# An mLSTM mixer whose head norm moves into the output weights and into its last product

## The chip, the cores and the metric

The kernel runs on one core of one Trainium2 chip. The metric is the device time of one execution in microseconds. The tensor engine (PE in the profile) has a queue of its own, as have VectorE (DVE), ScalarE (ACT), GpSimd (POOL) and SyncE (SP, which only issues loads here). They meet through semaphores alone, and each runs its own instructions in the order in which they are written. The matmuls are float32 products cut into parts: every operand x is held as a rounded high part and the rest, x = hi + lo, and three matmuls (hi·lo, lo·hi, hi·hi) stand for one.

## The reference, cut to what matters

The program is a stack of feed-forward blocks and four mixers over 256 tokens of width 1024. The change is in the first mixer, `mlstm_mixer`, which has 8 heads of 128 values each:

```python
h = h + 0.5 * swiglu(rmsnorm(h, ...), ...)               # block before
proj = rmsnorm(h, g) @ w_in                              # q, k, v, input and forget gates, output gate og
# ... decay weights W (256 x 256 per head, causal), num and den per head ...
h_out = num / jnp.maximum(jnp.abs(den), jnp.exp(-m_t))[..., None]
h_out = rmsnorm(h_out, g_head).reshape(B, T, H * M_DV)   # norm over the 128 values of each head
return (h_out * jax.nn.sigmoid(og)) @ w_out              # added to h; the next block follows
```

So for head j and token t the input of the last matmul is num · (share 1/max(|den|, floor)) · (root of the head) · g_head · sigmoid(og).

## The kernel before, in words

**Weights.** All weights pass through 7 slots in pieces of up to 128 x 2048. SP loads a piece when the slot is free (`used`, counted by PE after the last matmul on a piece); ACT writes its high part (`hi`, L1520, a copy to the rounded type), DVE its low part (`lo`, L2047, raw minus high). `split_to(p)` on either engine means "bring the parts of all pieces before p". Where it stands in an engine's program decides what waits behind 1.9 us (ACT) or 2.2 us (DVE) of it. The four pieces of the output matrix `a_w_out` are `first` to `first + 3`; piece i holds the rows of heads 2i and 2i + 1.

**Tokens.** There are two halves of 128 tokens, t = 0 and 1. Inputs of a matmul are turned by PE (a matmul with the identity), then ACT writes XH (`x_hi`) and DVE XL (`x_lo`).

**The first mixer on PE** (L1032 to L1126): chunks 0 to 2 of the projection; chunk 3 (96 matmuls of 256 columns, four column tiles m = 0 to 3); six small turns of the gate sums (`m_a`, `m_floor`, L1044); `rows_of_heads` (L1052), which DVE's `m_a` must precede; chunk 4; the scores of heads 0 to 3; the output gate's first product `og_products(5, 0, 7)`; the numerators of heads 0 to 3; scores 4 to 7; `og_products(6, 0, 7)`; numerators 4 to 7; the output gate of t = 1 (`og_products(5, 1, 2)` and `(6, 1, 3)`); `turn_heads(0)`, which waits for the finished heads of t = 0; and `out_stage`, eight parts of 12 matmuls of 512 columns (four pieces, t = 0 then t = 1), with `turn_heads(1)` after the second part. Then the second feed-forward block (`ffn1`) begins.

**On DVE** (L2341 to L2433): `values_in(2)`, `m_a`, the decay (L2353), the weights of each head (`m_weights`, L2369 and L2371), `numerators_in(g)` for four heads at a time (three small operations on shares and one product of 1024 elements from PSUM, L2387), `head_sums` (L2394: sums of the squares), `og_gain` (L2400: sigmoid(og) times g_head, 1024 elements), `mean_square` and `root` (11 small operations, L2077 and L2062 to L2072, for all 16 columns), `heads(t)` (L2408: eight products of 128 elements), and the `lo` pieces between them.

**On ACT** (L1707 to L1740): the decay's sigmoids, the `hi` pieces, `og_in` (the sigmoid of a gate product, L1723), `head_squares` (two Squares of 1024 elements, L1728), `x_hi` (L1548).

**On POOL**: the broadcast of g_head to 128 x 1024 (L645), and the causal zeros in the decay (L650).

Of the kernel before, what the change touches and what calls it, by code (L numbers as in the profile page):

```python
# [23 lines left out]
P = 128  # L24
# [82 lines left out]
def program(nc, a, out):  # L107
# [32 lines left out]
    NP = len(pieces)  # L140

    with ExitStack() as ctx:
# [60 lines left out]
        def carve(start, *sizes):  # L203
            views, at = [], start
            for n in sizes:
# [6 lines left out]
        m_qT, m_kT, m_v, m_og, m_E, m_g, m_tok, m_gain = carve(0, 1024, 1024, NT * HEADS * 129, 2048, HEADS * 384, 32, 80,  # L212
                                                                   1024)
# [9 lines left out]
        m_a = m_tok[:, 0:16].rearrange("p (t h) -> p t h", t=NT)  # L223
        m_floor = m_tok[:, 16:32].rearrange("p (t h) -> p t h", t=NT)
# [113 lines left out]
        og_dve = sem("og_dve")  # L338
        gain_in = sem("gain_in")
# [45 lines left out]
        roots = ["ffn0", "mlstm", "head", "ffn1", "kv", "keys", "kcmp", "nsa", "q0", "q1", "ffn3", "ln00", "ln01", "ckv",  # L385
# [241 lines left out]
        def _(pool):  # L627
# [17 lines left out]
            pool.dma_start(m_gain, a["a_g_head"].rearrange("l h d -> l (h d)")[0:1, :].to_broadcast([P, D])).then_inc(gain_in, 16)  # L645
# [28 lines left out]
        def _(pe):  # L674
# [57 lines left out]
            def turn_heads(t):  # L732

                pe.wait_ge(heads_ready, t + 1)
                for w in range(2):
                    for k in range(4):
                        last = tr(PS[:, turn_bank("mlstm_out", t, w), k * P:k * P + P],
                                  xs[:, t, (4 * w + k) * P:(4 * w + k) * P + P], ident)
                    last.then_inc(turned, 1)
# [195 lines left out]
            def out_stage(name, between=None):  # L935

                for t in range(NT):
                    if name != "mlstm_out":
                        pe.wait_ge(z_ready, 2 * zstage[name[:3]] + t + 1)
                    for i in range(4):  # L940
                        out_part(name, t, i)
                        if t == 0 and i == 1 and between:
                            between()
# [99 lines left out]
            chunk("mlstm", 3)  # L1043
            for name, sums in (("m_a", (grow[2], grow[0])), ("m_floor", (grow[1],))):  # L1044
                o = side(name)
                pe.wait_ge(side_src, src_no[name])
                for i, row in enumerate(sums):
                    for t in range(NT):
                        last = tr(o[:, 16 * i + 8 * t:16 * i + 8 * t + 8], row[:, t * P:t * P + P], con[0:HEADS, 0:HEADS])
                last.then_inc(side_ps, 1)  # L1050
# [41 lines left out]
            def og_products(c, t, bank):  # L1092

                n, end = stages["mlstm"][1][c][2], chunk_end("mlstm", c)
                for i, p in enumerate((end - 2, end - 1)):
# [6 lines left out]
                    if t == 1:  # L1102
                        last.then_inc(used, 1)
                if t == 0:
                    last.then_inc(og_ps, 1)
# [403 lines left out]
        def _(act):  # L1509
# [10 lines left out]
            def hi(p, n=PIECE):  # L1520

                act.wait_ge(landed[p % SLOTS], 32 * (p // SLOTS + 1))
                A(whi[:, p % SLOTS, 0:n], raw[:, p % SLOTS, 0:n], ACT.Copy).then_inc(hi_done, 1)  # L1523
# [15 lines left out]
            def x_hi(name, t):  # L1539

                for w in range(2):
# [171 lines left out]
            first = first_piece["mlstm_out"]  # L1713
# [11 lines left out]
            def head_squares(g, to):  # L1725
# [310 lines left out]
        def _(dve):  # L2036
# [391 lines left out]
            for w in range(2):  # L2428
                x_lo("mlstm_out", 0, w)
# [542 lines left out]
```

## Time and profile before

| | us |
|---|---|
| median of 3 runs (lowest, highest) | 1315.61 (1312.67, 1315.66) |
| span of the profiled execution | 1310.3 |
| PE busy in that span | 1270.2 |
| DVE busy | 873.9 |
| ACT busy | 613.6 |

The span runs from the first to the last instruction; the device time also holds what lies around it. The profiled execution's own device time is not printed: between its span and the three times lie 2.4 to 5.4 us. The first mixer takes some 110 us of the span, from about 203 to 317 us.

### The profile page before, as it was taken

The page shows a single profiled execution, that of the slowest core. Times are in us where ns is not written, and L with a number is a line of the kernel's source. Part 1 is how long each engine was busy: PE and PEld are TensorE (multiplying, and loading weights), DVE is VectorE, ACT ScalarE, POOL GpSimd, SP SyncE. Part 2 cuts the span into 40 slices and gives each one's busy share as a digit, 9 for nine tenths or more (in the row PEclk, how much of TensorE's full clock was granted, in tenths as well). Part 3 has the DMA queues.
Part 4 walks back from the last instruction along what each step waited for, and adds up shares of the span by engine and source line. Part 5 has one row for each costly group of instructions (what it writes and reads, how often), then busy time and mean ns, then how long its engine had stood idle before and what let it go on. Part 6 is the DMA issues. An engine that isn't in the chain of part 4 may idle for free.

```text
span 1310.3 us, 16491 instructions
## 1 busy us (share of the span) xinstructions
PE 1270.2 (97%) x6717; PEld 1077.6 (82%) x6717; DVE 873.9 (67%) x1312; ACT 613.6 (47%) x839; POOL 24.2 (2%) x37
## 2 busy tenths in 40 slices
PE   6999999989999999999999999999999999999997
PEld 5888888988788888878888886778888899988876
DVE  6655557885755556685657569856555567566896
ACT  6444346435434445444435357654444344544461
POOL 2000000100000000000000000000000000000000
PEclk9999999999999999999999989999999999999999
DMA  9655545443555556565665440065666686446401
GB/s 329 207 182 187 186 162 185 142 155 129 183 184 185 188 192 186 166 193 170 217 224 169 159 161 1 1 200 187 191 193 193 130 217 172 150 130 211 176 2 65
DMA packets 158812, 218.17 MB, mean 167 GB/s; under 512 B 8257, under 2 KB 110993, under 8 KB 158737
## 3 DMA queue, kind: packets, MB, share of 16 engines
q1 hardware_dynamic: 156880, 212.56, 51.2%
q0 software_dynamic: 1376, 3.71, 0.9%
q8 instruction: 53, 0.87, 0.3%
q10 hardware_dynamic: 480, 0.85, 0.2%
q14 instruction: 23, 0.18, 0.0%
HBM read 216.04 MB, written 1.05 MB: 166 GB/s over the span
## 4 chain that ended last, share of the span: by engine, by line
PE 82%; DVE 11%; issue 3%; ACT 2%; SPq 1%; DMA 1%; DVEq 0%
PE PS L686 23%; PE PS L689 23%; PE PS L687 23%; DVE wlo L2050 2%; PE PS L823 1%; PE PS L721 1%; PE PS L722 1%; ACT whi L1523 1%; PE PS L706 1%; PE PS L1300 1%; DVE arena L2639 1%; PE PS L728 1%; PE PS L1016 1%; SPq L591 1%; DVE XL L2090 1%
## 5 line engine op out<-in xcount | busy, mean ns | idle before, releaser
L2050 DVE TENSOR_TENSOR wlo<-raw,whi 128x2048 fp32r<-128x2048 f32 (+4 forms) x206 | 457.4, 2230 | 122.6 <-ACT whi L1523 121.8
L1523 ACT ACTIVATE whi<-raw 128x2048 fp32r<-128x2048 f32 (+4 forms) x206 | 381.4, 1863 | 63.4 <-DMA raw<-in_fox_w_in_dram 33.1
L686 PE MATMUL PS<-whi,XL 128*128 128x512 f32 (+3 forms) x992 | 385.8, 390 | 8.9 <-DVE scr L2152 3.8
L687 PE MATMUL PS<-wlo,XH 128*128 128x512 f32 (+3 forms) x992 | 379.8, 384 | 0.0
L689 PE MATMUL PS<-whi,XH 128*128 128x512 f32 (+3 forms) x992 | 265.0, 384 | 0.0
L686 PEld LDWEIGHTS PS<-whi,XL 128*128 128x128 f32 x992 | 187.3, 189 | 45.1 <-DVE scr L2152 4.9
L689 PEld LDWEIGHTS PS<-whi,XH 128*128 128x128 f32 x992 | 185.5, 190 | 35.5
L687 PEld LDWEIGHTS PS<-wlo,XH 128*128 128x128 f32 x992 | 187.4, 189 | 32.9
L1577 ACT ACTIVATE scr<-PS,rn 128x256 f32<-128x256 f32 x88 | 41.7, 474 | 225.2 <-PE PS L689 223.9
L686 PE MATMUL PS<-whi,GL 128*128 128x512 f32 x320 | 125.4, 392 | 0.0
L687 PE MATMUL PS<-wlo,GH 128*128 128x512 f32 x320 | 124.6, 389 | 0.0
L2149 DVE SCALAR_TENSOR_TENSOR scr<-PS,rn,scr 128x256 f32<-128x256 f32 x88 | 42.5, 483 | 92.8 <-ACT scr L1577 92.8
L1582 ACT ACTIVATE GH<-PS 128x512 fp32r<-128x512 f32 x40 | 23.9, 599 | 167.1 <-PE PS L823 167.1
L689 PE MATMUL PS<-whi,GH 128*128 128x512 f32 x320 | 98.7, 390 | 0.0
L686 PE MATMUL PS<-XH,wlo 128*128 128x256 f32 x320 | 81.4, 287 | 1.2 <-ACT xs L2017 1.2
L2158 DVE TENSOR_TENSOR GL<-PS,GH 128x512 fp32r<-128x512 f32 x40 | 27.7, 692 | 79.5 <-ACT GH L1582 79.4
L687 PE MATMUL PS<-XL,whi 128*128 128x256 f32 x320 | 80.2, 283 | 0.0
L689 PEld LDWEIGHTS PS<-whi,GH 128*128 128x128 f32 x320 | 60.1, 188 | 12.6
L687 PEld LDWEIGHTS PS<-wlo,GH 128*128 128x128 f32 x320 | 60.1, 188 | 12.1
L686 PEld LDWEIGHTS PS<-whi,GL 128*128 128x128 f32 x320 | 60.1, 188 | 12.2
L686 PEld LDWEIGHTS PS<-XH,wlo 128*128 128x128 f32 x320 | 61.3, 192 | 2.8 <-ACT xs L2017 2.0
L687 PEld LDWEIGHTS PS<-XL,whi 128*128 128x128 f32 x320 | 61.3, 192 | 0.1
(387 smaller groups left out, 1339.2 us busy)
## 6 DMA issues: line engine op xcount, KB each, us to landing
raw<-in_ffn_w_in_dram SPq DMA_DIRECT2D x174, 512.0 KB, 5.0
raw<-in_ffn_w_out_dram SPq DMA_DIRECT2D x88, 512.0 KB, 4.9
raw<-in_fox_w_in_dram SPq DMA_DIRECT2D x24, 512.0 KB, 7.9
raw<-in_a_w_in_dram SPq DMA_DIRECT2D x16, 512.0 KB, 4.6
raw<-in_dsa_w_in_dram SPq DMA_DIRECT2D x16, 512.0 KB, 6.0
raw<-in_kv_w_dram SPq DMA_DIRECT2D x12, 512.0 KB, 4.2
raw<-in_fox_w_in_dram SPq DMA_DIRECT2D x12, 344.0 KB, 5.0
raw<-in_a_w_out_dram SPq DMA_DIRECT2D x8, 512.0 KB, 4.9
```

The costliest lines, as they stand in the source:

```text
L591: sp.dma_start(dst[:, :, w, :], w_in[:, 4 * half:4 * half + 4, w, FC * i:FC * i + FC])\
L686: mm(o, xl, wh, start=start and i == 0, stop=False, skip_group_check=True)
L687: mm(o, xh, wl, start=False, stop=False, skip_group_check=True)
L689: last = mm(o, xh, wh, start=False, stop=stop and i == len(terms) - 1, skip_group_check=True)
L706: last = tr(PS[:, turn_bank(name, t, w), k * P:k * P + P], h[:, t, (4 * w + k) * P:(4 * w + k) * P + P], ident)
L721: mm(o, xh, wl, start=opens and i == 0 and j == 0, stop=False, skip_group_check=True)
L1523: A(whi[:, p % SLOTS, 0:n], raw[:, p % SLOTS, 0:n], ACT.Copy).then_inc(hi_done, 1)
L1577: A(ffe[:, t, :], PS[:, 4 + t, 0:FC], ACT.Sigmoid, scale=rn[:, t:t + 1]).then_inc(exp_done, 1)
L1582: A(to[:, :, :].rearrange("p k t -> p (k t)"), PS[:, 6, :], ACT.Copy).then_inc(gh_done, 1)
L2050: V.tensor_tensor(wlo[:, p % SLOTS, 0:n], raw[:, p % SLOTS, 0:n], whi[:, p % SLOTS, 0:n].bitcast(F32), ALU.subtract).then_inc(lo_done, 1)
L2149: V.scalar_tensor_tensor(out=g, in0=PS[:, 4 + t, 0:FC], scalar=rn[:, t:t + 1], in1=e, op0=ALU.mult, op1=ALU.mult).then_inc(silu_step, 1)
L2158: V.tensor_tensor(to[:, :, :], two(PS[:, 6, :]), hi_[:, :, :].bitcast(F32), ALU.subtract)\
```

## The change

The gain g_head is no longer multiplied into the gate. It scales the rows of the output matrix while its high and low parts are made (two operations of 1024 elements, one per head of the piece, in place of one of 2048), so `og_gain` and POOL's broadcast go. The squares are summed by ACT as it makes them (16 operations of 128 elements with an accumulator output, instead of two of 1024), so `head_sums` goes. The second four heads are squared from PSUM with the share as scale, and are no longer written out by `numerators_in(1)`: the last product reads them from PSUM, with share times root as its scalar. The root is taken per token half. The heads of t = 0 are turned four at a time: the first four in the middle of `og_products(6, 1, 3)`, the second four after the first part of `out_stage`; those of t = 1 after its third part. Some further steps are moved: `values_in(2)` ahead of the `lo` pieces, the gate sums' turns into chunk 3 (after tile m = 2), the parts of piece `first` ahead of the scores, and the first gate product ahead of a wait for the last decay. The banks into which heads are turned change from 4 to 7 to 2 to 5.

```diff
+    row_gains = {first_piece["mlstm_out"] + i: R_HEAD + 2 * i for i in range(4)}
...
             if name == "mlstm_out":
-                return 4 + 2 * t + w
+                return 2 + 2 * t + w
...
-            pool.dma_start(m_gain, a["a_g_head"].rearrange("l h d -> l (h d)")[0:1, :].to_broadcast([P, D])).then_inc(gain_in, 16)
...
+            def turn_heads(t, w):
+                pe.wait_ge(heads_ready, 4 if t else w + 1)
+                if t == 0:
+                    pe.wait_ge(og_act, 3 + w)
+                for k in range(4):
+                    last = tr(PS[:, turn_bank("mlstm_out", t, w), k * P:k * P + P],
+                              xs[:, t, (4 * w + k) * P:(4 * w + k) * P + P], ident)
+                last.then_inc(turned, 1)
...
+            pe.wait_ge(side_act, looks(side_no["m_M2"], "act"))
+            og_products(5, 0, 7)
             pe.wait_ge(side_act, looks(side_no["m_M3"], "act"))
-            og_products(5, 0, 7)
...
-            og_products(6, 1, 3)
-            turn_heads(0)
-            out_stage("mlstm_out", lambda: turn_heads(1))
+            og_products(6, 1, 3, lambda: turn_heads(0, 0))
...
+            out_stage("mlstm_out", {0: lambda: turn_heads(0, 1), 2: second_heads})
...
# ScalarE
+                if p in row_gains:
+                    for k in range(2):
+                        part = slice(D * k, D * k + D)
+                        last = A(whi[:, p % SLOTS, part], raw[:, p % SLOTS, part], ACT.Identity,
+                                 scale=par[:, row_gains[p] + k:row_gains[p] + k + 1])
...
             A(m_kT[:, 0:2, :], two(o), ACT.Copy).then_inc(chunk_act, 1)
+            first = first_piece["mlstm_out"]
+            split_to(first + 1)
             decay(2)
...
+                for j in range(4):
+                    hh, c = 4 * g + j, 8 * t + 4 * g + j
+                    if g == 0:
+                        src, by = xs[:, t, hh * P:hh * P + P], 1.0
+                    else:
+                        src, by = PS[:, 4 + j, t * T:t * T + P], m_shares[g][:, j, t:t + 1]
+                    last = A(m_squares[g][:, t, j * P:j * P + P], src, ACT.Square, scale=by, accum_out=ss[:, c:c + 1])
+                last.then_inc(head_sq, 1)
...
# VectorE
+                        last = V.scalar_tensor_tensor(
+                            out=wlo[:, p % SLOTS, part], in0=raw[:, p % SLOTS, part],
+                            scalar=par[:, row_gains[p] + k:row_gains[p] + k + 1],
+                            in1=whi[:, p % SLOTS, part].bitcast(F32), op0=ALU.mult, op1=ALU.subtract)
...
+            def head_root(t):
+                dve.wait_ge(head_sq, 3 + t)
+                mean_square(8, P, EPS, ss[:, 8 * t:8 * t + 8])
+                root(f"head{t}", 8, rr[:, 8 * t:8 * t + 8])
...
+                for g in range(2):
+                    if g:
+                        dve.wait_ge(head_sq, 4)
+                        fours = rr[:, 8 * t + 4:8 * t + 8]
+                        link(V.tensor_tensor(fours, fours, m_shares[1][:, :, t], ALU.mult))
+                    for j in range(4):
...
+                                                      in0=PS[:, 4 + j, t * T:t * T + P] if g else xs[:, t, cols],
+                                                      scalar=rr[:, c:c + 1], in1=m_og[:, t, cols],
...
+                    last.then_inc(heads_ready, 1)
...
-            head_sums(0)
+            shares(1).then_inc(m_out, 1)
+            dve.wait_ge(m_out, 2)
+            head_root(0)
+            heads(0)
+            x_lo("mlstm_out", 0, 0)
+            head_root(1)
             split_to(first + 3)
-            og_gain(0)
-            numerators_in(1)
-            head_sums(1)
-            mean_square(16, P, EPS)
-            root("head", 16)
-            heads(0)
-            og_gain(1)
-            for w in range(2):
-                x_lo("mlstm_out", 0, w)
+            x_lo("mlstm_out", 0, 1)
             heads(1)
```

DVE while PE works on chunk 3, kernel before (L2050 are `lo` pieces, L2287 is `values_in(2)`, L2343 and L2344 are `m_a`):

```order
L2050 TENSOR_TENSOR wlo<-raw,whi 128x2048 x2
L2287 TENSOR_SCALAR arena<-PS,r 128x4x128
L2343 TENSOR_SCALAR arena<-PS 128x16
L2344 TENSOR_SCALAR arena<-PS 128x16
L2050 TENSOR_TENSOR wlo<-raw,whi 128x1536 x2
```

The same place in the changed kernel (L2088 is `lo`, L2328 `values_in`, L2385 and L2386 `m_a`):

```order
L2328 TENSOR_SCALAR arena<-PS,r 128x4x128
L2088 TENSOR_TENSOR wlo<-raw,whi 128x2048
L2385 TENSOR_SCALAR arena<-PS 128x16
L2386 TENSOR_SCALAR arena<-PS 128x16
L2088 TENSOR_TENSOR wlo<-raw,whi 128x2048
L2088 TENSOR_TENSOR wlo<-raw,whi 128x1536 x2
```

One `lo` piece of 2048 has moved behind `m_a`.

DVE from the second four numerators to the heads of t = 0, kernel before (the root's ten operations are left out in the middle):

```order
L2050 TENSOR_TENSOR wlo<-raw,whi 128x2048
L2400 TENSOR_TENSOR arena<-arena 128x1024
...
L2386 RECIPROCAL arena<-arena 128x8
L2387 TENSOR_TENSOR xs<-PS,arena 128x4x2x128
L2394 TENSOR_REDUCE ss<-arena 128x2x4
L2077 TENSOR_SCALAR rv<-ss 128x16
...
L2072 SCALAR_TENSOR_TENSOR rr<-rt,ry 128x16
L2408 SCALAR_TENSOR_TENSOR xs<-xs,rr,arena 128x128 x8
L2400 TENSOR_TENSOR arena<-arena 128x1024
L2097 TENSOR_TENSOR XL<-PS,XH 128x4x128 x2
```

The same stretch in the changed kernel (L2082 is `lo` of an output piece, L2451 share times root, L2135 `x_lo`):

```order
L2082 SCALAR_TENSOR_TENSOR wlo<-raw,par,whi 128x1024 x2
...
L2428 RECIPROCAL arena<-arena 128x8
L2115 TENSOR_SCALAR rv<-ss 128x8
...
L2110 SCALAR_TENSOR_TENSOR rr<-rt,ry 128x8
L2456 SCALAR_TENSOR_TENSOR xs<-xs,rr,arena 128x128 x4
L2451 TENSOR_TENSOR rr<-rr,arena 128x4
L2456 SCALAR_TENSOR_TENSOR xs<-PS,rr,arena 128x128 x4
L2135 TENSOR_TENSOR XL<-PS,XH 128x4x128
```

Between the shares and the heads nothing is left but the root; the `lo` piece that stood there, and a second root, come behind.

PE at the end of the gate products, changed kernel (L736 are the turns of the heads; before, all eight stood in one row behind the last matmul of 384 columns):

```order
L687 MATMUL PS<-whi,XH 128x384 x4
L736 MATMUL PS<-con,xs 128x128 x4
L684 MATMUL PS<-whi,XL 128x384
...
L687 MATMUL PS<-whi,XH 128x384 x4
L684 MATMUL PS<-whi,XL 128x512
...
L687 MATMUL PS<-whi,XH 128x512 x2
L736 MATMUL PS<-con,xs 128x128 x4
```

Twelve gate matmuls now stand between the first four turns and the output products, and twelve output matmuls between the first and the second four turns.

## Rows read from the trace of the kernel before

**Rows 1.** Page, part 1: busy time, share of the span, instructions.
```profile
PE 1270.2 (97%) x6717; PEld 1077.6 (82%) x6717; DVE 873.9 (67%) x1312; ACT 613.6 (47%) x839; POOL 24.2 (2%) x37
```

**Rows 2.** PE's waits, 240 to 335 us: total, times, longest.
```profile
PE PS L737 <- DVE xs L2408: 2.5, 1, 2.5
PE PS L1058 <- DVE arena L2344: 1.0, 1, 1.0
PE PS L686 <- DVE XL L2097: 0.7, 1, 0.7
PE PS L686 <- ACT arena L1703: 0.6, 1, 0.6
PE PS L1087 <- DVE arena L2371: 0.4, 1, 0.4
PE PS L686 <- DVE xs L2387: 0.3, 1, 0.3
```

**Rows 3.** Windows: length, PE, PEld, DVE, ACT, POOL busy, PEclk, DMA share, GB/s.
```profile
287.00:290.00 3.00, 0.53 (x5) 0.40 (x5) 2.93 (x11) 0.58 (x1) 0.00 (x0) 0.99 1.01 348
...
292.00:296.00 4.00, 4.00 (x10) 3.17 (x11) 4.00 (x10) 1.70 (x1) 0.00 (x0) 0.50 0.66 212
296.00:300.00 4.00, 4.00 (x19) 3.24 (x18) 0.93 (x1) 0.00 (x0) 0.00 (x0) 0.90 0.00 0
```

**Rows 4.** PE in order of time: start, us, instruction, idle before.
```profile
232.54 0.28 PE L686 MATMUL PS<-XH,wlo 128*128 128x256 f32 x1
...
261.94 0.44 PE L686 MATMUL PS<-whi,XL 128*128 128x384 f32 x1 [0.62 <-ACT arena L1703]
262.22 0.33 PE L687 MATMUL PS<-wlo,XH 128*128 128x384 f32 x1
...
289.60 1.66 PE L737 MATMUL PS<-con,xs 128*128 128x128 f32 x8 [2.47 <-DVE xs L2408]
291.92 0.77 PE L686 MATMUL PS<-whi,XL 128*128 128x512 f32 x1 [0.65 <-DVE XL L2097]
...
298.38 0.39 PE L686 MATMUL PS<-whi,XL 128*128 128x512 f32 x1
298.61 0.39 PE L687 MATMUL PS<-wlo,XH 128*128 128x512 f32 x1
...
299.75 1.04 PE L737 MATMUL PS<-con,xs 128*128 128x128 f32 x8
```

**Rows 5.** DVE in order of time.
```profile
263.79 2.29 DVE L2050 TENSOR_TENSOR wlo<-raw,whi 128x2048 fp32r<-128x2048 f32 x1 [0.56 <-ACT whi L1523]
...
279.81 1.22 DVE L2400 TENSOR_TENSOR arena<-arena 128x1024 f32<-128x1024 f32 x1
...
285.18 0.17 DVE L2077 TENSOR_SCALAR rv<-ss 128x16 f32<-128x16 f32 x1
...
287.35 2.19 DVE L2408 SCALAR_TENSOR_TENSOR xs<-xs,rr,arena 128x128 f32<-128x128 f32 x8
```

**Rows 6.** ACT in order of time.
```profile
271.67 1.06 ACT L1728 ACTIVATE scr<-xs 128x1024 f32<-128x1024 f32 x1 [4.66 <-DVE xs L2387]
...
784.34 0.36 ACT L1862 ACTIVATE arena<-PS,nmin 128x128 f32<-128x128 f32 x1
784.68 0.37 ACT L1862 ACTIVATE arena<-PS,nmin 128x128 f32<-128x128 f32 x1
```

**Rows 7.** Groups by form: busy us, mean ns of one, idle before.
```profile
L1624 ACT ACTIVATE arena<-arena,nmin 128x128 f32<-128x128 f32 x16 | 6.2, 390 | 6.1 <-DVE nmin L2205 6.0
L2246 DVE SCALAR_TENSOR_TENSOR xs<-h,lns,arena 128x1024 f32<-128x1024 f32 x4 | 5.1, 1286 | 3.1 <-DMA arena<-in_ln_b_dram 3.0
L2371 DVE SCALAR_TENSOR_TENSOR arena<-PS,arena 128x128 f32<-128x128 f32 x8 | 2.7, 342 | 0.0
```

**Rows 8.** DVE and PE at the start of the next block, in order of time.
```profile
309.93 1.28 DVE L2120 SCALAR_TENSOR_TENSOR h<-PS,h 128x512 f32<-128x512 f32 x2
314.25 1.04 PE L706 MATMUL PS<-con,h 128*128 128x128 f32 x8
```

More of the change, by code:

```diff
@@ L223, in program @@
         m_a = m_tok[:, 0:16].rearrange("p (t h) -> p t h", t=NT)
+        m_shares = [m_tok[:, 32 + 8 * g:40 + 8 * g].rearrange("p (h t) -> p h t", h=4) for g in range(2)]
         m_floor = m_tok[:, 16:32].rearrange("p (t h) -> p t h", t=NT)
@@ L933, in out_part, with out_stage @@
                         last.then_inc(acc_done, 1)
-            def out_stage(name, between=None):
+            def out_stage(name, between={}):
                 for t in range(NT):
@@ L941, in out_stage @@
                         out_part(name, t, i)
-                        if t == 0 and i == 1 and between:
-                            between()
+                        if t == 0 and i in between:
+                            between[i]()
                         if t == 1 and i == 2 and name in then_turns:
@@ L1042, in _, with sums_turned @@
             chunk("mlstm", 2)
[L1043 to L1050, printed above, removed]
+            def sums_turned():
+                for name, sums in (("m_a", (grow[2], grow[0])), ("m_floor", (grow[1],))):
+                    o = side(name)
+                    pe.wait_ge(side_src, src_no[name])
+                    for i, row in enumerate(sums):
+                        for t in range(NT):
+                            last = tr(o[:, 16 * i + 8 * t:16 * i + 8 * t + 8], row[:, t * P:t * P + P], con[0:HEADS, 0:HEADS])
+                    last.then_inc(side_ps, 1)
+            chunk("mlstm", 3, None, {2: sums_turned})
             def rows_of_heads(name, j):
@@ L1103, in og_products @@
                         last.then_inc(used, 1)
+                    if between and i == 0:
+                        between()
                 if t == 0:
@@ L2049, in lo @@
                 dve.wait_ge(hi_done, p + 1)
+                if p in row_gains:
+                    for k in range(2):
+                        part = slice(D * k, D * k + D)
+                        last = V.scalar_tensor_tensor(
+                            out=wlo[:, p % SLOTS, part], in0=raw[:, p % SLOTS, part],
+                            scalar=par[:, row_gains[p] + k:row_gains[p] + k + 1],
+                            in1=whi[:, p % SLOTS, part].bitcast(F32), op0=ALU.mult, op1=ALU.subtract)
+                    last.then_inc(lo_done, 1)
+                    return
                 V.tensor_tensor(wlo[:, p % SLOTS, 0:n], raw[:, p % SLOTS, 0:n], whi[:, p % SLOTS, 0:n].bitcast(F32),
@@ L2396, in og_gain @@
-            def og_gain(t):
-                dve.wait_ge(og_act, 2 * t + 2)
-                dve.wait_ge(gain_in, 16)
-                V.tensor_tensor(m_og[:, t, :], m_og[:, t, :], m_gain, ALU.mult).then_inc(og_dve, 1)
-            def heads(t):
-                dve.wait_ge(og_dve, t + 1)
-                for hh in range(HEADS):
-                    cols = slice(hh * P, hh * P + P)
-                    c = 8 * t + hh
-                    last = V.scalar_tensor_tensor(out=xs[:, t, cols], in0=xs[:, t, cols], scalar=rr[:, c:c + 1],
-                                                  in1=m_og[:, t, cols], op0=ALU.mult, op1=ALU.mult)
-                last.then_inc(heads_ready, 1)
@@ L2412, in _, with first_numerators @@
-            split_to(first + 1)
+                return V.reciprocal(rd, rd)
+            def first_numerators():
+                link(shares(0))
+                V.tensor_tensor(xs[:, :, 0:512].rearrange("p t (h d) -> p t h d", h=4),
+                                PS[:, 4:8, :].rearrange("p h (t n) -> p t h n", t=NT)[:, :, :, 0:P],
+                                m_shares[0].rearrange("p h t -> p t h").unsqueeze(3).to_broadcast([P, NT, 4, P]),
+                                ALU.mult).then_inc(m_out, 1)
```

69 lines of the change are left out of this document (34 added, 35 removed).

## The prediction

> **What bounds the kernel now.** First the busy shares: PE is busy for 97% of the span [rows 1]. So a change that leaves PE's instructions as they are, as this one does (the same products, 16 turns of 128 x 128 in another place), can give back only PE's idle time and time at a low clock. The page's groups don't show where that lies, so I read the waits next, in the stretch of the first mixer. PE waits there six times, 5.5 us in all [rows 2]: 2.5 for the heads of t = 0 (L737), 1.0 for `m_a` (L1058), 0.7 for XL ahead of the first output product, 0.6 for the last decay ahead of the first gate product, 0.4 for the first head's weights (L1087), 0.3 for the first numerators. The third view is the windows [rows 3]: the longest wait falls in 287 to 290 us; in 292 to 296 PE ran at half the clock (0.50, its 1.2 GHz level), in 296 to 300 at 0.90 on average. The fourth is PE in order of time [rows 4], which puts a price on this. The first eight turns took 1.66 us, the second eight 1.04. The 24 products between 291.92 and 299.75 took 7.83 us; at the spacing of 0.23 us that they have once the clock is back (298.38 to 298.61) they would take 5.4. So the wait of 2.47 cost 0.6 + 2.4 = 3.0 us more through the clock. No other wait of rows 2 was followed by this.
>
> **The profiled execution and the median.** The sums are made in the span of 1310.3 us. The median of 1315.6 is 5.3 above it, the lowest time 2.4. I take off from the median what I take off from the span.
>
> **What each removed wait is worth.** The five waits that the change aims at: 2.47 + 1.03 + 0.65 + 0.62 + 0.41 = 5.2 us. Each also costs PE its pipelining: a matmul of 0.39 us starts 0.23 after the one before, so 0.16 us of overlap is lost, and the first after a wait is longer (0.44 against 0.33 [rows 4]); 0.25 each, 1.2 in all. With the clock's 3.0 the most that can come is 9.4 us. The wait of 0.3 for the first numerators stays: same operations, same order.
>
> **Do the waits really go?** I lay the changed kernel out with PE as the clock, from the start of chunk 3 at 232.5 [rows 4], without waits unless one is found. The spacing is 0.23 us for 512 columns [rows 4], and in proportion 0.17 for 384, 0.12 for 256 and 0.11 for 128, by the eight turns at 299.75 (1.04 less 0.16 of overlap, over 8). Three tiles of chunk 3 end at 241.3, the six small turns at 242.0, the fourth tile at 244.9; rows of heads 245.8, chunk 4 257.5, rows of heads 258.4, scores 260.2, gate product 264.3, numerators and scores 268.7, the kept wait 269.0, gate product 273.2, numerators 276.0, 36 gate products 282.0, four turns and 12 gate products 284.5, output part 287.2, four turns and two parts 293.1, eight turns 294.0.
>
> *The gate sums.* `m_a` comes behind one `lo` piece, where two stood (2.2 us each [rows 5]), and PE turns the sums inside chunk 3, at 241.3. `m_a` ends at 243.4, PE asks for it at 244.9. Behind it the moved piece (second half of chunk 4) is ready at 245.6, asked for at 247.3. The wait of 1.03 goes.
>
> *The early output piece.* Parts of piece `first` (2.2 to 2.5 us on DVE) move ahead of the key copy L2360, into DVE's idle time before it. Queued behind it is that copy, which the scores wait for: it ends at 258.3, PE is there at 258.4. No slack, but no cost; were it 0.5 late, 0.5 is lost. In exchange the head weights start as soon as the decays are done (261.9 instead of 266.0), so the 0.41 goes; and the gate product no longer waits for the fourth decay, so the 0.62 goes.
>
> *The squares.* ACT now runs 16 Squares with accumulator. Nearest rows: L1862, the same size from PSUM with an accumulator, starts every 0.34 us (784.34 to 784.68 [rows 6]); L1624 from SBUF lasts 0.39, and its readout lies beside the next [rows 7]. Lower bound 0.34; upper bound one old Square of 1024 elements, 1.06 [rows 6]. I take 0.38 from SBUF, 0.36 from PSUM. The first eight (3.1 us) and a `hi` piece (now 2 x about 1.05, by L1728's 1.06 for 1024 elements) stand ahead of `og_in(6, 0)`, which numerator 7 waits for: from 269.0, 3.1 + 2.1 + 0.5 gives 274.8; PE asks at 275.2. Hidden with 0.4 to spare.
>
> The Trainium skill (VectorE: DVE Perf Modes, on the TRN2 errata) says that ScalarE pays a fixed 224 cycles per instruction from SBUF and 172 from PSUM, and advises against tiles under 512 elements, which speaks against 16 small squares for two large ones. By its formula one costs 0.29 us (352 cycles at 1.2 GHz) before the readout of the accumulator. The rows' 0.34 to 0.39 hold the readout, so the sum would be the same; the advice would only bite if ACT had no idle time here.
>
> *The chain to the heads.* Before: `lo` piece, `og_gain` 1.2, numerators, Square 1.1 [rows 6], `head_sums` (1024 elements like `og_gain`), root of 11 operations from 285.18 to 287.35 (2.2), eight products 2.2 [rows 5]. Now from numerator 7's end at 276.0: shares 0.6, four PSUM squares 1.5, root 2.2 (its operations are bound by their fixed part: 0.17 us for 16 columns), four products 1.1: 281.7. PE asks after 36 gate products of 0.17, at 282.0. Slack 0.3. The second four need the other squares (279.9), the share product (0.2) and four products from PSUM (L2371 from PSUM 0.34, like L2408 from SBUF): 283.0, asked for at 287.2. The first output product asks for XL at 284.5, there at 284.0. So 2.47 and 0.65 go, and with them the half clock: PE has no wait over 0.4 us from 232 to past 320.
>
> *The gained parts* of the output pieces on DVE: nearest rows 1.22 (L2400, 1024 elements [rows 5]) and 1.29 (L2246, three operands [rows 7]), less 0.1 of overlap: 2.3 to 2.5 a piece instead of 2.2. Piece `first + 3` stands behind both heads(1) and the second root; DVE works without a pause from 278.3 to about 294.3. PE asks for it at 294.0. Here I expect a wait of 0.3 us (0 to 0.9 by these bounds).
>
> The Trainium skill (same page, same section) gives VectorE 120 fixed cycles from PSUM against 58 from SBUF. The eight products that now read PSUM would be longer by 62 cycles, 0.065 us, each: 0.5 us on DVE's full stretch, and the wait here 0.8. The rows don't bear it out (0.342 from PSUM, 0.348 from SBUF), so I leave it out of the sum.
>
> *The next block.* Before, DVE's updates of h begin at 309.93 and end 3.0 us ahead of PE's turns at 314.25 [rows 8]. PE gains on DVE, since the three `lo` pieces between still follow the `hi` pieces. I get 304.6 for DVE and 305.2 for PE, so the cover shrinks to under a us.
>
> *POOL's broadcast* of 0.5 MB runs early, at 32 us, where no wait of PE is; nothing.
>
> Sum: 9.4 - 0.3 (last output piece) - 0.3 (half of the chance that one of the three places with under 0.4 us of slack is missed by 0.6) = 8.8 us. Nothing behind the first mixer is tied to absolute time, so the gain stays.
>
> **The rivals.**
> - *DVE becomes the bound at the seams.* If gained parts and products are at their upper bounds, waits of 0.9 at the last output piece, 0.5 at the key copy, 0.3 at the first turns and up to 1 at the turns of the next block come back, none long enough to lower the clock if the rows are a guide (1.03 did not). Gain about 9.4 - 2.7 = 6.7: 1309. For it: DVE's full stretch; against: every price has a near row.
> - *The long wait only shrinks.* If squares take 0.6 each, numerator 7 waits 1.3 and the first turns 0.6. If a wait near 2 remains (at 0.75), the clock falls again: gain 9.4 - 3.0 - 2.5 - 1 = 3: 1312.6.
> - *Slower: the squares on ACT.* It is one mechanism: ACT's queue holds eight squares ahead of `og_in(6, 0)` and eight ahead of `og_in(5, 1)`. At 1.0 us a square, near the upper bound, numerator 7 waits 8 x 0.62 - 0.4 = 4.5 us and the turns of the first heads, which also wait for `og_in(5, 1)`, 3.3. Each wait is longer than the 2.47 that brought half clock, so 3.0 comes twice. Against the 9.4: 7.8 + 6.0 = 13.8, so 4.4 slower: 1320. It decides from about 0.8 us a square. Against it: rows 6 and 7 have the same size at less than half of that.
> - *It doesn't do what it says: given back later.* The weights for the next block come with all DMA queues busy (share 1.01 [rows 3]). If their loads, not PE, set its start, PE only waits there instead. Against: the loads follow PE's own `used`, and four pieces of 1 MB, whose slots come free from 278 on, take 3 us each at 350 GB/s: the last lands at about 292 and is wanted at 308. No change: 1315.5.
>
> **How the numbers follow.** Forecast 0.63 (1304.5 to 1308.8), DVE at the seams 0.20, the wait that shrinks 0.08, slower 0.04, given back 0.05. The likeliest gives 1315.6 - 8.8 = 1306.8. Range 1303 to 1312: the low end is the full 9.4 and the 3 us by which the three times before differ; the high end takes in the seams and most of the shrunken wait. Under 0.3% (3.9 us) a measurement of this kernel can't tell a change from none. Faster by more: 0.63 + 0.20 + 0.02 = 0.85. Within: 0.06 + 0.05 = 0.11. Slower: 0.04.
>
> **What would show it.** Right: PE clock 1.00 through 287 to 300; no PE wait over 0.5 us on the heads' turns, on `m_a` or on the decay; PE's first output product about 7 us earlier; Squares of 128 elements starting every 0.34 to 0.40 us. Wrong: a PE wait of over 2 us anywhere between 260 and 310; numerator 7 waiting for ACT; a stretch of PE at 0.50; or a shorter mixer and a next block that waits for DMA.

## The result, and the profile after

The changed kernel takes 1302.5 us (median of four, 1301.3 to 1303.1); the kernel before took 1314.9 in the runs beside it (1312.7 to 1315.7). The ratio of the runs is 0.9921, with a 95% interval of 0.9903 to 0.9939 (the quotient of the two medians, 0.9906, lies inside it). Later, on another chip with more runs, it was 1303.2 against 1312.1: 0.993 (0.9916 to 0.9945). So it is faster by 0.7 to 0.8%, and the two intervals leave 0.6 to 1.0%. The span went from 1310.3 to 1299.6.

Page, part 1, of the kernel after. PE has the same 6717 matmuls [rows 1], is busy for 3.8 us less (for the most part the half clock, which had stretched the mixer's matmuls by about 2.8, below) and idle for less; DVE and ACT hardly changed.

```profile
PE 1266.4 (97%) x6717; PEld 1075.7 (83%) x6717; DVE 870.9 (67%) x1324; ACT 617.9 (48%) x873; POOL 24.5 (2%) x36
```

PE's waits, 230 to 345 us, after (the stretch that holds those of [rows 2]): us in total, times, longest.

```profile
PE PS L684 <- DVE scr L2190: 0.9, 1, 0.9
PE PS L684 <- DVE xs L2433: 0.3, 1, 0.3
```

All five waits that the prediction set out to remove are gone. The 0.3 for the first numerators stayed, as forecast. The 0.9 lies in the next block, after 318 us, and stood there before the change too: the stretch of [rows 2] holds this seventh wait as well, 0.89 us at 330.71, which those rows leave out. The windows over the heads, which answer to [rows 3], have PE busy throughout at a granted clock of 1.00:

```profile
280.00:283.00 3.00, 3.00 (x21) 2.97 (x20) 2.33 (x9) 0.60 (x1) 0.00 (x0) 1.00 0.95 297
283.00:286.00 3.00, 3.00 (x15) 2.48 (x14) 2.69 (x12) 0.58 (x1) 0.00 (x0) 1.00 1.01 340
286.00:290.00 4.00, 4.00 (x21) 3.32 (x20) 3.85 (x12) 2.68 (x3) 0.00 (x0) 1.00 1.09 358
```

PE in order of time, for [rows 4]. Subtract 1.95 us from any time of before to compare: chunk 3 starts that much earlier, for a reason that lies at the start of the program (below).

```profile
230.59 0.28 PE L684 MATMUL PS<-XH,wlo 128*128 128x256 f32 x1
...
258.44 0.45 PE L684 MATMUL PS<-whi,XL 128*128 128x384 f32 x1
...
280.75 0.60 PE L736 MATMUL PS<-con,xs 128*128 128x128 f32 x4
...
283.28 0.39 PE L684 MATMUL PS<-whi,XL 128*128 128x512 f32 x1
...
291.98 1.03 PE L736 MATMUL PS<-con,xs 128*128 128x128 f32 x8
292.77 0.47 PE L684 MATMUL PS<-whi,XL 128*128 128x512 f32 x1
```

The first output product starts 8.6 us earlier than in [rows 4], and the eight last turns 7.8. Less the shift that is 6.7 (about 7 was the sign of being right) and 5.8.

DVE and ACT, after, for [rows 5] and [rows 6]: the root of t = 0 begins at 276.95, behind the last of its PSUM squares; the products of `heads` that read their numbers from PSUM cost the same as those from SBUF.

```profile
276.95 0.17 DVE L2115 TENSOR_SCALAR rv<-ss 128x8 f32<-128x8 f32 x1 [1.64 <-ACT arena L1753]
...
279.04 1.14 DVE L2456 SCALAR_TENSOR_TENSOR xs<-xs,rr,arena 128x128 f32<-128x128 f32 x4
...
280.29 1.13 DVE L2456 SCALAR_TENSOR_TENSOR xs<-PS,rr,arena 128x128 f32<-128x128 f32 x4
282.02 0.69 DVE L2135 TENSOR_TENSOR XL<-PS,XH 128x512 fp32r<-128x512 f32 x1 [0.61 <-ACT XH L1566]
...
290.20 2.47 DVE L2082 SCALAR_TENSOR_TENSOR wlo<-raw,par,whi 128x1024 fp32r<-128x1024 f32 x2
```
```profile
267.51 0.31 ACT L1753 ACTIVATE scr<-xs 128x128 f32<-128x128 f32 x1 [3.99 <-DVE xs L2433]
...
267.82 0.29 ACT L1753 ACTIVATE scr<-xs 128x128 f32<-128x128 f32 x1
268.02 0.19 ACT L1753 ACTIVATION_READ_ACCUMULATOR scr<-xs 128x1 f32 x1
268.11 0.29 ACT L1753 ACTIVATE scr<-xs 128x128 f32<-128x128 f32 x1
...
275.34 0.37 ACT L1753 ACTIVATE arena<-PS,arena 128x128 f32<-128x128 f32 x1 [2.73 <-DVE arena L2428]
...
275.70 0.36 ACT L1753 ACTIVATE arena<-PS,arena 128x128 f32<-128x128 f32 x1
```

A square starts every 0.29 us from SBUF and every 0.34 to 0.36 from PSUM.

**One measure for every trace below.** The *mixer stretch* is PE's time from the start of chunk 3 (232.54 in [rows 4]) to the first turn of gated values in the next feed-forward block (336.30 there): before 103.76, after 325.82 - 230.59 = 95.23. So the mixer gave 8.53 us, where 8.8 was forecast. The span fell by 10.7. Of the other 2.2, 1.98 had arisen by 33 us, at the first such turn of the first block (33.34 before, 31.36 after).

### The profile page after: what moved, and what is told of

Read it like the earlier page. It is cut to its first block, busy times and chain, and to the rows that moved or that the text cites. A ratio compares the mean times of both kernels' runs of the same rounds, so it can differ in the third digit from the quotient of the medians.

```text
span 1299.6 us, 16537 instructions
## 1 busy us (share of the span) xinstructions
PE 1266.4 (97%) x6717; PEld 1075.7 (83%) x6717; DVE 870.9 (67%) x1324; ACT 617.9 (48%) x873; POOL 24.5 (2%) x36
## 4 chain that ended last, share of the span: by engine, by line
PE 86%; DVE 9%; issue 2%; ACT 2%; SPq 1%; DMA 1%; DVEq 0%
PE PS L684 25%; PE PS L687 25%; PE PS L685 24%; PE PS L822 1%; PE PS L719 1%; PE PS L720 1%; DVE wlo L2088 1%; PE PS L726 1%; PE PS L704 1%; PE PS L1015 1%; PE PS L1311 1%; DVE arena L2685 1%; SPq L590 1%; DMA raw<-in_ffn_w_out_dram 1%; DVE d_work L2934 1%
## 5 line engine op out<-in xcount | busy, mean ns | idle before, releaser
L2088 DVE TENSOR_TENSOR wlo<-raw,whi 128x2048 fp32r<-128x2048 f32 (+4 forms) x202 | 448.2, 2229 | 121.2 <-ACT whi L1541 120.5
L1541 ACT ACTIVATE whi<-raw 128x2048 fp32r<-128x2048 f32 (+4 forms) x202 | 373.8, 1862 | 61.9 <-DMA raw<-in_fox_w_in_dram 32.7
L684 PE MATMUL PS<-whi,XL 128*128 128x512 f32 (+3 forms) x992 | 384.5, 388 | 6.6 <-DVE scr L2190 2.7
L684 PEld LDWEIGHTS PS<-whi,XL 128*128 128x128 f32 x992 | 186.4, 188 | 42.0 <-DVE scr L2190 3.9
L684 PE MATMUL PS<-whi,GL 128*128 128x512 f32 x320 | 125.4, 392 | 0.0
L684 PE MATMUL PS<-XH,wlo 128*128 128x256 f32 x320 | 81.5, 287 | 1.2 <-ACT xs L2046 1.2
L684 PEld LDWEIGHTS PS<-whi,GL 128*128 128x128 f32 x320 | 60.1, 188 | 12.2
L684 PEld LDWEIGHTS PS<-XH,wlo 128*128 128x128 f32 x320 | 61.3, 191 | 2.9 <-ACT xs L2046 2.0
```

The costliest lines, as they stand in the source:

```text
L684: mm(o, xl, wh, start=start and i == 0, stop=False, skip_group_check=True)
L2088: V.tensor_tensor(wlo[:, p % SLOTS, 0:n], raw[:, p % SLOTS, 0:n], whi[:, p % SLOTS, 0:n].bitcast(F32), ALU.subtract).then_inc(lo_done, 1)
```

## The experiments

Spans are of one profiled execution each. From the first block's turn to chunk 3, all fourteen traces agree within 0.05 us (199.18 to 199.23), so the mixer stretch can be read to better than 0.1: the two traces of before differ by 0.02, the two of after by 0.04. The two ends of the program can't: up to the first turn took 31.3 to 33.3, and all behind the stretch 972.6 to 976.0.

The far end goes with the clock. Between the mixer and the last 15 us, where all but root first have the same instructions, early moves only and delay four show no half clock and took 972.6 and 972.7; the four traces with one such stretch of 6.8 us took 973.7 to 974.0, and the seven with two stretches 974.8 to 976.0. (Root first has one of 3.4 and took 972.7, with its own saving in it.) Which of them a trace has does not follow the kernel: after has one, after again two.

| kernel | up to first turn | mixer stretch | waits in it beyond those of after | rest of the difference |
|---|---|---|---|---|
| before | 33.34 | 103.76 | 5.18 | 3.35 |
| before, again | 31.34 | 103.78 | 5.25 | 3.30 |
| after | 31.36 | 95.23 | 0 | 0 |
| after, again | 31.85 | 95.19 | 0 | 0 |
| broadcast back | 31.45 | 95.21 | 0 | 0 |
| early moves only | 31.48 | 100.71 | 3.51 | 1.97 |
| heads only | 31.88 | 97.89 | 2.53 | 0.13 |
| delay, three | 31.29 | 96.96 | 1.49 | 0.24 |
| delay, four | 31.32 | 98.17 | 2.76 | 0.18 |
| two waits | 31.45 | 101.87 | 3.45 | 3.19 |
| one longer | 31.92 | 102.04 | 4.01 | 2.80 |
| turns together | 31.79 | 97.06 | 1.28 | 0.55 |
| gain in the gate | 32.19 | 96.26 | 0.79 | 0.24 |
| root first | 31.57 | 94.04 | -0.87 | -0.32 |

The last column is the stretch less 95.23 less the waits: refilling PE, and the clock.

**1. The changed kernel again.**

> The changed kernel once more, with a second profile. My theory: the first mixer alone gave 8.5 us (PE from the start of chunk 3 to the first turn of the next block's gates: 95.2 us against 103.8), and the 2 us by which the changed kernel was already ahead at 33 us are chance, since no changed instruction of PE lies there. Then 95.2 within 0.2 again, and the stretch 0 to 33 us may fall either way by 2 us; ratio 0.990 to 0.994. Rival (the start belongs to the change): the changed kernel is again 2 us ahead at 33 us, and PE never drops to half clock at 28 us.

Measured: stretch 95.19, ratio 0.993; the first turn came at 31.85, with the clock at 1.00 from 10 to 34 us. That is as the theory has it for the mixer. For the start it leaves the rival standing, since 31.85 is again 1.5 ahead of the one trace of before; experiment 5 decides it.

**2. The broadcast back.** The gains are loaded again, and only waited for, not used:

```diff
+            pool.dma_start(m_gain, a["a_g_head"]...to_broadcast([P, D])).then_inc(gain_in, 16)
...
                 dve.wait_ge(og_act, 2 * t + 2)
+                dve.wait_ge(gain_in, 16)
```

> The changed kernel with POOL's 0.5 MB broadcast of the head gains put back into the start (loaded, not used). Theory: it costs nothing: time within 1 us of the changed kernel beside it, mixer stretch 95.2. Rival (the broadcast held the loads at the start up): 2 us slower than the changed kernel, PE at half clock near 28 us as in the kernel before.

Measured: 1302.7 against 1303.2 for the changed kernel on the same chip, stretch 95.21, first turn at 31.45. The broadcast costs nothing, as predicted, and its absence did not bring the 2 us at the start.

**3. The early moves alone.**

> The kernel before with only the moves in the early part: values of a chunk taken before its split piece, the sums turned inside chunk 3, the first output piece split ahead of the key copy, the gate product behind M2. Theory: the waits of 1.03, 0.62 and 0.41 us go, 2.1 us, with next to nothing for refills; the heads are not faster, so their wait stays near 2.5 and the half clock behind it too: mixer stretch 103.8 - 2.1 = 101.7, about 2 us faster than before. Rival (the waits are one chain: what is removed early comes back at the heads): the wait for the heads grows to 4.5 and the stretch stays at 103.8. By my recorded sum with 0.25 a refill it would be 2.8.

Measured: 1307.1 against 1312.1, ratio 0.9966 (0.9953 to 0.9979); the stretch is 100.71, so 3.05 gained where I expected 2.1. The waits on `m_a`, the decay and the first weights are gone, and the one for the heads kept its size:

```profile
PE PS L737 <- DVE xs L2419: 2.4, 1, 2.4
PE PS L686 <- DVE XL L2103: 1.1, 1, 1.1
PE PS L686 <- DVE scr L2158: 0.9, 1, 0.9
PE PS L686 <- DVE xs L2398: 0.3, 1, 0.3
```

So the rival of one chain falls: what was taken away early did not come back at the heads, apart from 0.4 us at XL. The surplus over 2.1 is in the clock: the waits in the stretch are 1.67 less than before, and the other 1.38 stands in the last column of the table, nearly all of it clock (the three refills saved are about 0.13). Windows of this kernel show PE at half clock from 288.0 to 291.4 only, 3.4 us, where it was 6.8 in the kernel before ([rows 3] has 0.50 throughout 292 to 296):

```profile
284.00:288.00 4.00, 1.40 (x10) 1.15 (x10) 3.76 (x9) 1.77 (x3) 0.00 (x0) 1.00 1.07 358
288.00:292.00 4.00, 4.00 (x12) 3.13 (x11) 4.00 (x10) 1.11 (x1) 0.00 (x0) 0.57 0.66 210
292.00:296.00 4.00, 4.00 (x24) 3.35 (x23) 0.44 (x1) 0.50 (x2) 0.00 (x0) 1.00 0.00 0
```

**4. The heads alone.**

> The changed kernel with the early moves undone: only the heads' part stays (gain in the output weights, squares with accumulator on ACT, root and gate by half, turns within the last gate product). Theory: the waits of 1.03, 0.62 and 0.41 are back, no wait for the heads over 0.5 and no half clock: stretch 95.2 + 2.1 = 97.3, about 6.4 faster than before. If both parts add, this and the early moves alone sum to 8.5. Rival (the later start of the head weights, by the `first` piece of 2.3 us on DVE, reaches the heads): wait of over 1 us at the heads' turns, stretch 99 or more.

Measured: 1306.3 against 1312.1, ratio 0.9954 (0.9938 to 0.9971); stretch 97.89, 5.87 gained, no half clock. There was no wait for the heads, so the rival falls. The wait for the first weights was 0.9 instead of 0.4, since the late `first` piece has its gain now and the weights stand behind it: most of the 0.6 by which it missed 97.3. DVE's half of the piece is 0.2 longer than in [rows 5], and ACT's high part comes later, so DVE waits 0.84 for it and not 0.56:

```profile
262.60 2.48 DVE L2081 SCALAR_TENSOR_TENSOR wlo<-raw,par,whi 128x1024 fp32r<-128x1024 f32 x2 [0.84 <-ACT whi L1537]
```

The two parts give 3.05 + 5.87 = 8.92, and 8.53 together. So the early moves are worth 3.05 on the kernel before, some 1.25 of it by a shorter half clock, and 8.53 - 5.87 = 2.66 on top of the heads' part.

**5. The kernel before again**, for the start.

> The kernel before once more, for a second trace. At 33 us it was 1.5 to 2.0 us behind the four other kernels (33.3 against 31.4 to 31.9 at the first turn of the first block's gates), and one of those four has the broadcast and none of the heads' part. Theory: that was chance, it comes at 31.4 to 31.9 now; the mixer stretch is 103.8 again. Rival: it belongs to the kernel before, 33.3 again.

Measured: first turn at 31.34, stretch 103.78. The 2 us at the start were chance. Windows of the first trace of before and then of this one: in the first PE had waited 1.97 us for gated values, and ran at half clock from 27.1 to 30.6; here the same wait was 1.3, and the clock stayed at 1.00.

```profile
24.00:27.00 3.00, 1.03 (x6) 0.70 (x5) 2.62 (x4) 2.27 (x3) 0.00 (x0) 1.00 1.10 349
27.00:31.00 4.00, 4.00 (x12) 3.13 (x11) 3.96 (x4) 1.07 (x2) 0.00 (x0) 0.57 1.08 376
```
```profile
24.00:27.00 3.00, 1.74 (x8) 1.19 (x7) 2.64 (x4) 2.27 (x3) 0.00 (x0) 1.00 1.10 348
27.00:31.00 4.00, 4.00 (x19) 3.31 (x18) 3.96 (x5) 0.66 (x2) 0.00 (x0) 1.00 1.07 374
```

**6 and 7. A wait of chosen length at the first turns.** On DVE, before the root of t = 0, n operations that keep the gate's values (n = 3, then 4; one trace each):

```diff
             dve.wait_ge(m_out, 2)
+            dve.wait_ge(og_act, 2)
+            for _ in range(n):
+                link(V.tensor_tensor(m_og[:, 0, :], m_og[:, 0, :], m_og[:, 0, :], ALU.max))
             head_root(0)
```

> The changed kernel with three extra 1024-element operations (1.2 us each; they leave the values as they are) on DVE before the root of t = 0. DVE has 1.64 us idle there and the turns have about 0.6 of slack, so PE waits about 1.4 us at the first turns. Theory (the clock falls only behind a long wait): stretch 95.2 + 1.4 + at most 0.6 at XL = 96.6 to 97.2, clock 1.00 throughout. Rival (any wait of over 1 us at this place costs the half clock): 98 or more.

> The same with four: PE waits about 2.6 us at the first turns. Theory: half clock behind it as in the kernel before: 95.2 + 2.6 + 1.7 to 3.0 = 99.5 to 100.8. Rival (the half clock came from the two waits of 2.5 and 0.65 close together, or was chance): clock stays 1.00, 97.8.

Measured: 1.49 us of wait and a stretch of 96.96; 2.76 us and 98.17. The first is as expected, the second is not: my theory that a wait of this length always brings half clock fell, and the rival's 97.8 with the clock at 1.00 is near. Windows of the kernel with four:

```profile
281.00:284.00 3.00, 0.40 (x4) 0.40 (x5) 2.73 (x14) 0.00 (x0) 0.00 (x0) 1.00 0.90 269
284.00:288.00 4.00, 4.00 (x23) 3.69 (x22) 3.52 (x17) 1.19 (x2) 0.00 (x0) 1.00 1.00 329
```

**8 and 9. Two waits close together, or one longer.** The second theory, from the traces so far, was that the second wait (0.65 us, at XL [rows 2]) was needed too.

> The changed kernel with four extra operations on DVE before the root of t = 0 and two more before its first XL (values kept): PE waits 2.8 us at the first turns, as it did with four alone, and 1.6 more at the first output product, 2.7 us of work later. In both traces of the kernel before and in the one with only the early moves, the half clock came behind two waits close together (2.5 and 0.65, or 2.4 and 1.1); a single 2.8 left the clock alone. Theory: two waits close together bring it: 95.2 + 2.8 + 1.6 = 99.6 for the waits and 1.3 to 3.0 on top, 101 to 102.6. Rival (the place or chance decides): clock 1.00, 99.6.

> The changed kernel with five extra operations before the root of t = 0 and none at XL: one wait of 4.0 us. If the sum of idle time in such a stretch decides (2.5 + 0.65 is more than 2.8), the half clock comes here too: 95.2 + 4.0 + 1.3 to 3.0 = 100.5 to 102.2. If it takes two waits, the clock stays 1.00: 99.2 to 99.4.

Measured: 101.87 and 102.04, both with half clock, and both in the range of their theories. But PE in the kernel with two waits, and the windows behind it, show that the theory of two waits falls as well:

```profile
283.73 0.66 PE L736 MATMUL PS<-con,xs 128*128 128x128 f32 x4 [2.75 <-DVE xs L2456]
288.29 0.77 PE L684 MATMUL PS<-whi,XL 128*128 128x512 f32 x1 [0.70 <-DVE XL L2135]
```
```profile
281.00:283.00 2.00, 0.00 (x0) 0.00 (x0) 1.73 (x11) 0.00 (x0) 0.00 (x0) 1.00 0.99 327
283.00:285.00 2.00, 1.27 (x9) 1.27 (x10) 1.93 (x9) 0.58 (x1) 0.00 (x0) 1.00 1.03 317
285.00:287.00 2.00, 2.00 (x8) 2.00 (x7) 1.97 (x2) 0.02 (x1) 0.00 (x0) 0.50 1.08 374
```

The second wait is 0.70 and not the planned 1.6, since PE at half clock comes to it later (3.9 us behind the start of the first turns, where after has 2.5). The clock fell at 285.0, 2.6 us before the second wait begins. Up to there this kernel and the one with four operations do the same on PE, with waits of 2.75 and 2.76, and one lost its clock and the other kept it. In both traces of the kernel before the clock also fell ahead of the wait for XL. So neither the length of a wait of this size nor a second one decides; a wait of 2.45 to 2.76 us brought the half clock four times out of five, the one of 4.01 once out of once, waits of up to 1.5 in this stretch never.

The traces hold the same case at a second place, in instructions that the change leaves alone. Four of them come there at a clock of 1.00 and wait 2.74 to 2.76 us. (In the other ten the clock had fallen already at some point from 750 us on, and this wait is at most 1.6.) In early moves only and delay four the clock stays; in heads only and root first it falls 1.5 us after the wait has ended. Early moves only, then root first:

```profile
781.22 0.73 PE L1286 MATMUL PS<-GH 128*128 128x512 f32 x2 [2.74 <-ACT arena L1868]
783.00:787.00 4.00, 4.00 (x40) 3.63 (x40) 3.74 (x8) 4.00 (x23) 0.00 (x0) 1.00 0.00 0
```
```profile
774.57 0.73 PE L1292 MATMUL PS<-GH 128*128 128x512 f32 x2 [2.75 <-ACT arena L1893]
776.00:780.00 4.00, 4.00 (x27) 3.78 (x24) 2.90 (x5) 3.91 (x21) 0.00 (x0) 0.57 0.00 0
```

What decides between them isn't settled by these runs. The Trainium skill (TensorE: Matmul & The Clock Gate, Part 1) says that the hardware's watch over PE runs free, and is not reset when a kernel starts; that would make one and the same wait fall differently from run to run. The pair 2.75 and 2.76 and the four waits at the second place agree with it; none of these runs set out to test it, so it is not shown.

**10. The turns together again.** The part "turns inside the last gate product" is undone:

```diff
-            og_products(6, 1, 3, lambda: turn_heads(0, 0))
+            og_products(6, 1, 3)
+            turn_heads(0, 0)
+            turn_heads(0, 1)
...
-            out_stage("mlstm_out", {0: lambda: turn_heads(0, 1), 2: second_heads})
+            out_stage("mlstm_out", {2: second_heads})
```

(and ACT takes the last gate piece ahead of both XH).

> The changed kernel with the eight turns of t = 0 together, behind the whole gate product, as they stood before the change. The heads are there (280.1 and 281.4 against 283), so there is no wait for them; XH (0.6 us) and XL (0.7) of the first four then have only the 0.5 us of the other four turns beside them. Theory: one new wait of 0.7 to 1.3 us at the first output product, clock 1.00: stretch 95.9 to 96.5. Rival (the turns inside the gate product are worth nothing): 95.2.

Measured: 97.06, so moving the turns is worth 1.83 us, more than my 0.7 to 1.3. The wait at the first output product is 0.58. Two that I had missed add 0.32 (the second turns overwrite the bank that ACT's gate piece is read from) and 0.38 (the last output piece, which is pushed back behind them).

```profile
PE PS L684 <- DVE scr L2191: 0.9, 1, 0.9
PE PS L684 <- DVE XL L2136: 0.6, 1, 0.6
PE PS L684 <- DVE wlo L2083: 0.4, 1, 0.4
PE PS L684 <- DVE xs L2434: 0.3, 1, 0.3
PE PS L736 <- ACT arena L1744: 0.3, 1, 0.3
```

**11. The gain in the gate again.** Output pieces unscaled, the broadcast back, and on DVE:

```diff
+            og_gain(0)
             head_root(0)
             heads(0)
...
+            og_gain(1)
             heads(1)
```

> The changed kernel with the head gains multiplied into the gate on DVE again (two operations of 1.2 us, and the broadcast) and the output pieces unscaled. Theory: the first of the two falls into DVE's idle 1.64 us before the root, so there is no wait for the heads; the second stands in DVE's full stretch ahead of the last output piece, which now ends at about 293.5 against 292.8 of PE: one wait of 0.7 us, stretch 95.9. Rival (the gain products hold up the heads): a wait of 1 us or more at the first turns, 96.4 or more.

Measured: 96.26, one new wait of 0.8 at the last output piece (`wlo`) and none for the heads, as the theory said; the stretch is 0.36 over its 95.9, by 0.1 of wait and 0.24 of refill. The fold into the weights is worth 1.0 us, not at the heads but 12 us later. What else is in the heads' part (the sums and squares on ACT, the second four read from PSUM, the root by halves) was not run by itself.

**12. The root first.** The largest wait left near the mixer is the 0.87 at the first gated products of the next block. In the changed kernel DVE and PE stand there so:

```profile
302.14 1.28 DVE L2158 SCALAR_TENSOR_TENSOR h<-PS,h 128x512 f32<-128x512 f32 x2
...
312.84 2.16 DVE L2128 SCALAR_TENSOR_TENSOR XL<-PS,par,XH 128x128 fp32r<-128x128 f32 x8 [3.81 <-ACT XH L1563]
314.91 0.16 DVE L2115 TENSOR_SCALAR rv<-sn 128x2 f32<-128x2 f32 x1
```
```profile
303.78 1.03 PE L704 MATMUL PS<-con,h 128*128 128x128 f32 x8
...
320.22 0.50 PE L684 MATMUL PS<-whi,XL 128*128 128x512 f32 x1 [0.87 <-DVE scr L2190]
```

The gated values need a root that DVE works out from 314.91, behind its last XL, after 3.81 us of idle time. I moved the root into that idle time, in both blocks that follow an output stage:

```diff
+                if name in norms and out:
+                    squares(name, 1)
                 x_hi(name, 1)
-                if name in norms:
+                if name in norms and not out:
                     squares(name, 1)
...
                 if name in outs:
+                    if then in norms:
+                        token_root(then)
                     for w in range(2):
                         x_lo(then, 1, w)
```

> The changed kernel, with the root of the token norm of the two blocks that follow an output product (second and fourth feed-forward) worked out before the last halves of x are split: ACT squares t = 1 before its last XH, DVE takes the root before its last XL. The root then runs in DVE's idle 3.8 us ahead of 312.8. Theory: the waits of 0.87 and 0.9 us at the first gated products go, each stage that much shorter: 1.7 us faster than the changed kernel, ratio to the kernel before about 0.9915 where the changed one has 0.993. Rival (XL of t = 1 comes late, since it stands behind the root): a new wait at the last products of t = 1, no gain.

Measured: 1300.5 (1299.2 to 1301.2) against 1310.6 of before; the ratio is 0.992 (0.9906 to 0.9935), the one expected 0.9915. The stretch is 94.04, 1.19 shorter (0.87 of wait and 0.32 beside it), the rival's new wait did not come, and of PE's three waits of this kind (L684 on L2190) in the whole trace only the one at the start is left. DVE, root and XL of this kernel:

```profile
310.46 0.17 DVE L2117 TENSOR_SCALAR rv<-sn 128x2 f32<-128x2 f32 x1 [1.22 <-ACT xs L1555]
...
313.12 2.16 DVE L2130 SCALAR_TENSOR_TENSOR XL<-PS,par,XH 128x128 fp32r<-128x128 f32 x8 [0.64 <-ACT XH L1563]
```

XL starts at its old time behind chunk 3 (313.12 against 312.84, with the whole run 0.21 later). The gain over the changed kernel shows in the trace; between the total times the intervals overlap, so there it is not shown apart from chance.

## Why the prediction was right, and where it was not

The median came 0.5 us under the low end of 1303.0, and 4.3 under the forecast of 1306.8. The mixer's own gain, which was all that the sum dealt with, was 8.53 against 8.8. The rest can't lie in the mixer; it lies in the ends of the program, and in the baseline. The median of before that the forecast started from was 1315.6, while on two other chips the same kernel had medians of 1312.1 and 1310.6; the profiled trace of before held 2 us at the start that its second trace did not; and the far end differs by 3.4 us with stretches of half clock that no kernel owns. How near a single pair of medians comes to the forecast is therefore in part chance: on the chip of the later runs they differ by 8.9, on this one by 12.4. The step that failed is "I take off from the median what I take off from the span", with its range: that was to hold "the 3 us by which the three times before differ", and three times could not show that the kernel before scatters from 1308.9 to 1315.8.

Term by term:
- *Five waits, 5.2.* Right to the tenth; each went, and experiments 3 and 4 show which part took which.
- *Refill, 5 x 0.25 = 1.2.* Mis-sized. The last column of the table prices it where the clock stayed up: 0.18 to 0.24 for a single wait ahead of turns or output products, and 0.13 for the three early waits together. For the five that is about 0.6.
- *Half clock, 3.0.* What is left of 3.35 is about 2.8. The long stretches in the kernels with two waits and one longer cost nearly the same, 3.19 less two refills and 2.80 less one; the short one 1.97 less two refills, about 1.5. The size was right; that "the wait of 2.47 cost" it is true only as a chance. The rival that expected half clock "if a wait near 2 remains" rested on the same step, and the wait of 2.76 without it shows that the step was too firm.
- *Seams, -0.6.* Too cautious: neither the wait at the last output piece nor a missed seam came. That piece ends at 292.67 and PE asks at 292.77. Refill and seams cancel, so the sum came out closer than its terms.
- *The laid-out schedule.* Less the shift of 1.95, PE was due at the first turns at 280.05 and came at 280.75; heads were due at 279.75 and came at 280.18. Both were late, so the slack of 0.3 became 0.57.
- *The squares.* Taken at 0.38 and 0.36, measured 0.29 and 0.34. The rival with 1.0 us a square is refuted. The 0.29 lies below the 0.34 to 0.40 that were named as a sign of being right. The Trainium skill (VectorE: DVE Perf Modes, TRN2 errata) gives 224 and 172 fixed cycles, by estimate 0.29 us from SBUF, as measured, but 0.25 from PSUM; here those from PSUM were the slower ones (0.37 for one). The Trainium skill's advice of 512 elements and more (same page and section) did not bite: ACT was idle for 4.0 us before the squares. Those from PSUM also take their scale from a column of numbers, which the runs do not separate from the source. [Rows 7] speak for the column, though for another function: L1624 takes a column, reads SBUF and lasts 0.39.
- *VectorE's reads from PSUM.* Eight products took 345 ns each from PSUM and 348 from SBUF, so it was right to leave out of the sum the 62 extra cycles from PSUM that the Trainium skill gives (VectorE: DVE Perf Modes, TRN2 errata).
- *The gained pieces* took 2.47 to 2.48, and 2.76 for piece `first`; forecast 2.3 to 2.5. There ACT's part was ready, and each of the two products took 1.42 instead of 1.28. POOL was busy with the causal zeros beside them (248.70 to 254.88), and in before the two pieces of 1536 beside the zeros took 3.72 against 3.43 for the two ahead of them. That POOL is the cause was not tested. The longer piece still cost no wait: it had idle time behind it.
- *POOL's broadcast, nothing.* Right, by experiment 2.
- *Given back later.* It wasn't: "cover under a us" at the next block's turns holds (DVE is done at 302.14 + 1.28 = 303.42, PE is there at 303.78), with no wait.

## What to carry to other kernels

When PE is 97% busy, price a change by PE's waits one by one and ignore the busy time that it moves between DVE and ACT; then move work only into idle time whose end you have found. Of the two parts here the early moves cost nothing but order, and gave 2.7 of the 8.5. A wait of PE of 2.5 us may cost another 1.5 to 2.8 us through the clock, so such waits are worth more than their length, but only on average. And before a time is taken as a baseline to 0.3%, look at the two ends of a second trace of it.

## What the runs showed of the hardware

- One wait of PE at the same place, 2.75 and 2.76 us long: once the granted clock fell from 1.00 to 0.50 1.3 us after its end, once it never fell. At a second place, with waits of 2.74 to 2.76, it fell in two traces and stayed in two. The half clock of this mixer lasted about 6.8 us in four traces (cost: about 2.6 to 2.8) and 3.4 in one (about 1.5), and 3.4 at the start of the program where it came. In the trace with the wait of 4.01 the clock fell during the wait.
- A Square of 128 elements with its accumulator starts every 0.29 us from SBUF and, with a scale from a column, every 0.34 from PSUM; the readout (0.19 to 0.23) lies beside the next.
- DVE products of 128 elements from PSUM cost the same as from SBUF (345 and 348 ns).
- Beside POOL's causal zeros DVE's products of 1024 elements took 1.42 us instead of 1.28, and pairs of 1536 3.72 instead of 3.43; the cause was not tested.
